# Order of loads and stores on SyncE's DMA queue in a PEER block: the activation store ahead of the next weight load

## The reference

```python
def chunk(ht):                       # 128 tokens
    q = (ht @ w_q).reshape(PEER_CHUNK, PEER_HEADS, 2, PEER_HALF)
    s = jnp.einsum('thpc,hpnc->thpn', q, subkeys)
    sv, si = lax.top_k(s, PEER_TOPK)
    ...                              # top 16 of the 16 x 16 sums per head -> expert, gate
    ue = u[expert]
    ve = v[expert]
    act = jax.nn.gelu(jnp.einsum('thkd,td->thk', ue, ht), approximate=False)
    return jnp.einsum('thk,thkd->td', (gate * act), ve)
```

## Time and profile before

| | us |
|---|---|
| median of 3 runs | 2909.25 |
| lowest, highest | 2909.18, 2910.72 |
| the profiled execution | 2909.18 |
| its span, first to last instruction | 2907.4 |
| TensorE (PE) busy | 2806.9, 97% |
| VectorE (DVE) busy | 1906.2, 66% |
| GpSimd (POOL) busy | 1549.0, 53% |
| ScalarE (ACT) busy | 901.7, 31% |

### The profile page before, as it was taken

The page is one execution under the profiler, slowest core; times in us unless marked ns, Lnnn a source line. Parts: engine busy times, 40 slices in busy tenths (PEclk is TensorE's granted clock), DMA queues, the critical chain, the costliest instruction groups (busy, mean ns, idle before and its releaser), DMA issues.

```text
span 2907.4 us, 44634 instructions
## 1 busy us (share of the span) xinstructions
PE 2806.9 (97%) x16719; PEld 2372.6 (82%) x16719; DVE 1906.2 (66%) x4442; ACT 901.7 (31%) x1750; POOL 1549.0 (53%) x1088
## 2 busy tenths in 40 slices
PE   7999989999999999999999998999999999999998
PEld 6777667999999999899999998666767766767675
DVE  6022363799888999999999743655555555555554
ACT  4223341322222222366666522222222222222222
POOL 1111020455666677755555563866656566666662
PEclk9999989999999999999999999999999999999999
DMA  3100031345777788899999996989999999899996
GB/s 137 44 30 30 23 131 73 102 144 208 264 271 281 262 274 289 293 360 373 379 381 381 369 344 255 338 303 336 332 332 337 334 322 327 314 333 319 324 324 231
DMA packets 300377, 763.51 MB, mean 263 GB/s; under 512 B 21456, under 2 KB 136528, under 8 KB 297424
## 3 DMA queue, kind: packets, MB, share of 16 engines
q0 software_dynamic: 110592, 402.70, 38.3%
q1 hardware_dynamic: 189648, 359.13, 34.7%
HBM read 669.47 MB, written 92.27 MB: 262 GB/s over the span
## 4 chain that ended last, share of the span: by engine, by line
PE 74%; DVE 8%; POOL 3%; DMA 1%; issue 1%; ACT 1%; ACTq 0%; DVEq 0%; POOLq 0%
PE bank L1832 30%; PE bank L1488 26%; PE wide L1852 6%; PE bank L1796 5%; PE bank L1707 3%; PE bank L1724 2%; POOL w_lo L602 1%; DVE u_row L1309 1%; DVE eq L1296 1%; DMA w_raw<-in_u 1%; PE bank L1733 1%; POOL u_row L611 1%; DVE eq L1294 1%; DVE route L1298 1%; POOL v_row L662 1%
## 5 line engine op out<-in xcount | busy, mean ns | idle before, releaser
L662 POOL DMA_INDIRECT v_row<-in_v,ids_t x384 | 381.6, 994 | 391.2 <-PE wide L1852 283.0
L1488 PE MATMUL bank<-h_hi,w_hi 128*128 128x320 f32 (+1 forms) x2400 | 574.3, 321 | 16.2 <-POOL w_lo L602 13.9
L1488 PE MATMUL bank<-h_hi,w_lo 128*128 128x320 f32 (+1 forms) x2400 | 557.1, 313 | 0.0
L1488 PE MATMUL bank<-h_lo,w_hi 128*128 128x320 f32 (+1 forms) x2400 | 557.1, 313 | 0.0
L1405 DVE TENSOR_TENSOR a_lo<-prod,a_hi 128x384 fp32r<-128x384 f32 (+1 forms) x256 | 264.0, 1031 | 445.4 <-ACT a_hi L969 445.2
L602 POOL TENSOR_TENSOR w_lo<-w_raw,w_hi 128x1024 fp32r<-128x1024 f32 x144 | 367.3, 2551 | 337.7 <-ACT w_hi L889 205.2
L1309 DVE CUSTOM_DVE_ANT_0 u_row<-wide,u_row 128x1024 f32<-128x1024 f32 x384 | 450.2, 1220 | 76.5 <-DMA u_row<-in_u_rows,ids 74.4
L611 POOL DMA_INDIRECT u_row<-in_u_rows,ids x384 | 390.7, 1017 | 113.4 <-issue 73.8
L1488 PEld LDWEIGHTS bank<-h_hi,w_hi 128*128 128x128 f32 x2400 | 400.5, 190 | 23.0 <-POOL w_lo L602 15.0
L1832 PE MATMUL bank<-v_hi,a_hi 128*128 128x512 f32 x1272 | 407.6, 402 | 10.4 <-POOL v_lo L651 5.3
L1488 PEld LDWEIGHTS bank<-h_lo,w_hi 128*128 128x128 f32 x2400 | 406.8, 189 | 4.0
(11 more groups left out here) (211 smaller groups left out, 3480.2 us busy)
## 6 DMA issues: line engine op xcount, KB each, us to landing
w_raw<-in_u SPq DMA_DIRECT2D x128, 512.0 KB, 5.4
v_raw<-in_v SPq DMA_DIRECT2D x32, 2048.0 KB, 19.6
act_d<-act_st SPq DMA_DIRECT2D x128, 320.0 KB, 5.3
g_d<-g_st SPq DMA_DIRECT2D x20, 2048.0 KB, 9.4
a_raw<-act_d SPq DMA_DIRECT2D x32, 768.0 KB, 8.1
g_raw<-g_d SPq DMA_DIRECT2D x32, 768.0 KB, 11.8
w_raw<-in_w_q SPq DMA_DIRECT2D x32, 512.0 KB, 3.4
a_raw<-act_d SPq DMA_DIRECT2D x32, 512.0 KB, 10.5
```

The source lines that it names most:

```text
L662: nc.gpsimd.indirect_dma_start(v_row[k % RING][:, :], None, v_rows, bass.IndirectOffsetOnAxis(ids_t[:, t, TW * s + c:TW * s + c + 1], 0)). ...
L1488: ins = pe.matmul(banks[h][:, 0:n], lhs[:, part], rhs[:, k, h * n:(h + 1) * n], start=(k == 0 and lhs is lhs_hi and rhs is h_hi), stop=(k ...
```

## The change

In SP's program a store used to be one item behind: for each t it issued the load of item t + 2 and then the store of item t - 1. Now it issues the load of item t + 2 and then the store of item t. The strip's store still stands right behind the activation store of the strip's second item. The loads of v, a and g stand behind both stores of their pair of items, one item later than before. The strips' part of SP's program is now a loop instead of 40 written-out items.

```diff
             load_item(0)
             load_item(1)
             for t in range(2 * BODY1):
                 load_item(t + 2)
-                if t:
-                    store_item(t - 1)
+                if query_of(t) is None:
+                    sp.wait_ge(act_done, 2 * t + 2)
+                    sp.dma_start(act_d[chunk_of(t)], act_st[:, t % 2, :]).then_inc(act_out[t % 2], 16)
+            def first_half(it, last=False):
+                for s in range(2):
+                    if not last:
+                        sp.wait_ge(lo_done, it * 2 + (W_U0 + s + 1))
+                        sp.dma_start(w_raw[:, s, :], u_d[it * 2 + (2 + s - Q_PIECES)]).then_inc(raw_in[s], 16)
+                    sp.wait_ge(act_done, it * 4 + (2 * s + 2))
+                    sp.dma_start(act_d[it * 2 + (s - Q_PIECES)], act_st[:, s, :]).then_inc(act_out[s], 16)
             with sp.Fori(BODY1, B0) as it:
-                for s in range(2):
-                    sp.wait_ge(lo_done, it * 2 + (W_U0 + s + 1))
-                    sp.dma_start(w_raw[:, s, :], u_d[it * 2 + (2 + s - Q_PIECES)]).then_inc(raw_in[s], 16)
-                    sp.wait_ge(act_done, it * 4 + 2 * s)
-                    sp.dma_start(act_d[it * 2 + (s - 1 - Q_PIECES)], act_st[:, 1 - s, :]).then_inc(act_out[1 - s], 16)
-            for t in range(2 * B0, 2 * C0):
-                load_item(t + 2)
-                store_item(t - 1)
-                if t % 2 == 0 and t > 2 * B0:
-                    store_strip(t // 2 - B0 - 1)
+                first_half(it)
+            with sp.Fori(0, PAIRS) as it:
+                for s2 in range(2):
+                    first_half(it * 2 + (B0 + s2))
+                    sp.wait_ge(gs_done, it * 16 + (8 * s2 + 8))
+                    sp.dma_start(g_d[it * 2 + s2], g_st[:, s2, :, :]).then_inc(g_out[s2], 16)
...
             for it in range(C0, ITEM_BODIES):
-                for t in (2 * it, 2 * it + 1):
-                    if t + 2 < ITEMS:
-                        load_item(t + 2)
-                    store_item(t - 1)
-                    if t == 2 * C0:
-                        store_strip(STRIPS - 1)
+                first_half(it, last=it == ITEM_BODIES - 1)
                 k = it - (ITEM_BODIES - 6)
                 if k in (0, 1):
                     load_v(0, k)
...
-            store_item(ITEMS - 1)
```

More of the change, by code:

```diff
@@ L472, in load_item @@
                 load_piece(W_U0 + t, u_d[chunk_of(t)] if hp is None else wq_d[hp])
[L474 to L478, removed]
             load_item(0)
@@ L483, in _ @@
                 load_item(t + 2)
-                if t:
-                    store_item(t - 1)
-            with sp.Fori(BODY1, B0) as it:
-                for s in range(2):
-                    sp.wait_ge(lo_done, it * 2 + (W_U0 + s + 1))
-                    sp.dma_start(w_raw[:, s, :], u_d[it * 2 + (2 + s - Q_PIECES)]).then_inc(raw_in[s], 16)
-                    sp.wait_ge(act_done, it * 4 + 2 * s)
-                    sp.dma_start(act_d[it * 2 + (s - 1 - Q_PIECES)], act_st[:, 1 - s, :]).then_inc(act_out[1 - s], 16)
-            def store_strip(st):
-                sp.wait_ge(gs_done, 8 * st + 8)
-                sp.dma_start(g_d[st], g_st[:, st % 2, :, :]).then_inc(g_out[st % 2], 16)
-            for t in range(2 * B0, 2 * C0):
-                load_item(t + 2)
-                store_item(t - 1)
-                if t % 2 == 0 and t > 2 * B0:
-                    store_strip(t // 2 - B0 - 1)
+                if query_of(t) is None:
[8 more added lines that the diff above has]
+                    sp.dma_start(act_d[it * 2 + (s - Q_PIECES)], act_st[:, s, :]).then_inc(act_out[s], 16)
+            with sp.Fori(BODY1, B0) as it:
+                first_half(it)
[4 more added lines that the diff above has]
+                    sp.dma_start(g_d[it * 2 + s2], g_st[:, s2, :, :]).then_inc(g_out[s2], 16)
             def load_v(g, s):
```

## The result

The changed kernel takes 2943.57 us (median of 4, 2940.6 to 2946.18) against 2909.22 (median of 4, 2906.33 to 2910.72). The ratio is 1.0119, 95% interval 1.0101 to 1.0137. It is slower, as forecast, but by 34 us and not by 12, and outside the range (2909 to 2932). The profiled execution took 2943.35, its span is 2941.6.

What follows compares the result with a forecast made beforehand. The prediction took TensorE to bound the item stage, with late transfers costing only past their slack. Plain items 0, strips 3.1 and v loads 8.5 made 11.6 us on 2909.18, so 2920.8 us, range 2909 to 2932.

Steps and rivals of the forecast that it cites:

- The bound and the thresholds: Item stage: TensorE bounds; L889 lateness costs only beyond 2.73 us in plain items, 3.36 us in strips.
- Plain items, cost 0: Plain items: the weight load makes L889 at most 2.5 us late, under 2.73, so nothing is lost.
- The rival by which they gain: Plain items before the strips: gathered rows land sooner, TensorE's 13.9 us of waiting shrink; 2902 us; 6%.
- The v loads, +8.5: End of item stage: weight loads behind two 2 MB v loads come late; 5.3 + 4.2 - 1.0 = +8.5 us.
- Its first term: First v load: the load behind it makes L889 7.99 us late, costing TensorE 5.26 us.
- Its second term: Second v load: the load behind it makes L889 late, loss 2.9 or 5.6 us, taken as 4.2.
- The strips, +3.1: Strips: loads behind strip stores cost 2.4 us in the first, 0.7 in the second, 0 in a settled one.
- Every strip stalls: Strips: each load 1.5 us later still, strips cost 10 us instead of 3.1, total 2928 us; 18%.
- The load overtakes: Loads right behind 2 MB transfers: they land in about 6 us, all terms vanish, 2908.2 to 2909.2 us; 18%.

Runs made afterwards that it cites:

- the run of its own: Kernel before with only the last 20 items, including the v, a and g loads, in the new order; 2912.08 us, ratio 1.0027.
- the strips' experiment, the first experiment: Kernel before with only the 20 strips in the new order, written out without a loop on SyncE; 2943.49 us, ratio 1.0133.
- new order, gathers pinned: Kernel before with only strips in the new order, plus GpSimd issuing an item's four gathers there before waiting for w_hi; 2991.51 us, ratio 1.0286.
- its control: Kernel before with only GpSimd's order in the strips changed, gathers issued before its wait for w_hi; 2993.05 us, ratio 1.0293.

## Why the prediction was wrong

*The bound and the thresholds.* Right. In the strip shown above L878 (once L889) was due when the gelus were through; its usual start is 0.63 us after theirs, at 1397.55. It started at 1402.73, x = 5.18, and 5.18 - 3.36 = 1.82 is TensorE's idle time of 1.80. The run with L889 behind a gate copy tests the same threshold.

*Plain items, cost 0.* Right: alone they measure a ratio of 0.9998. The rival by which they gain doesn't hold either.

*The v loads, +8.5.* The sum is near (+7.6 alone), but partly by luck. Its first term holds: the step that took 14.63 us for the load behind a v load from the earlier trace rows found 14.20, L889 waited 7.56 us where it was to be 7.99 late, and TensorE stood 4.79 where 5.26 was forecast (4.50 in the run of its own). Its second term, 4.2 us, measures nothing. The load behind the second v load was usable 1788.54 - 1775.45 = 13.09 us after it and not 14.63 to 17.37, and the item it was for came later than forecast, because TensorE ran at half its clock behind the first wait; L889 waited 1.39, under the threshold of 2.73. That slower stretch, 2.3 us, is what the forecast lacked, and it fills about half of the second term.

*The strips, +3.1.* Wrong, and this is the miss. The step that failed is "the load that is now issued 0.4 us behind the strip store lands when the load that followed that store landed before". For a settled strip that would have been 12.7 us after the store, x = 2.67 and under the threshold by 0.7. It came at a median 14.1 in the changed kernel and 14.8 in the strips' experiment, over the threshold in every settled strip of the latter, and a settled strip lost 1.8 to 2.0 us in the mean. The step kept the rest of the traffic where it stood, and it moves. This is GpSimd before the change (after the w_lo of the item, its gathers; strip store at 1402.46):

```profile
1393.60 2.39 POOL L602 TENSOR_TENSOR w_lo<-w_raw,w_hi 128x1024 fp32r<-128x1024 f32 x1 [3.31 <-DVE gate_j L1371]
...
1399.89 0.99 POOL L611 DMA_INDIRECT u_row<-in_u_rows,ids  x1 [0.31 <-issue]
```

and after it (strip store at 1411.52):

```profile
1403.93 2.38 POOL L591 TENSOR_TENSOR w_lo<-w_raw,w_hi 128x1024 fp32r<-128x1024 f32 x1 [5.94 <-ACT w_hi L878]
1406.46 1.23 POOL L600 DMA_INDIRECT u_row<-in_u_rows,ids  x1
...
1410.72 0.94 POOL L600 DMA_INDIRECT u_row<-in_u_rows,ids  x1 [0.30 <-issue]
```

A late L889 makes w_lo late, GpSimd issues its four gathers (2 MB) behind w_lo, and the last of them now starts 0.8 us ahead of the strip store, where it was 2.6. By this account they are still in the DMA engines' queues when the strip store comes, the load behind it lands later, and the next L889 is late again.

Medians of the settled strips, us; the last column is from the strip store's issue to its landing:

| run | last gather ahead of the store by | last load ahead by | store lands in |
|---|---|---|---|
| kernel before | 2.58 | 6.44 | 9.4 |
| strip store behind the load | 3.06 | 0.48 | 11.1 |
| kernel before, w_lo and gathers held back | 0.73 | 0.85 | 11.4 |
| new order, gathers ahead narrow | 2.55 | 10.6 | 7.8 |
| new order, gathers pinned | 3.08 | 12.5 | 8.6 |
| new order, gathers behind narrow | 1.35 | 11.6 | 12.4 |
| new order, L889 behind L917 | 0.68 | 10.6 | 11.5 |

In the four rows with the new order no load is near, and the store lands 3 to 5 us later where whole gathers start 0.7 to 1.4 us ahead of it than where they start 3.1 us ahead (in strips that are 3 to 4 us longer, though) or are narrow. For the strips' experiment and the changed kernel the profile has no landing, but it has the DMA engines' packets: the store's last packet ends 11.8 and 11.0 us after its issue, 8.9 before, and in that time 1.64 and 1.48 MB of gathers are moved, 0.97 before. The time order agrees as well. The first strip of the strips' experiment has no late L889 ahead of it, and its L889 comes 14.23 us after the store, earlier than the 15.79 of the forecast. From the second strip on it comes later than forecast: 15.83 for 14.15, then 13.7 to 15.6 for 12.7.

Taking the gathers ahead out takes the loss to zero, taking those behind out only from 39 to between 24 and 26 us. That the loop as a whole keeps itself up is put together from these links. The run that was to cut it by itself, with the gathers pinned, couldn't be read by its time since its control moved, and this was not tried in another way.

*The rivals.* "Every strip stalls" is what happened. It was given 18% and 10 us, and the strips cost 39. I gave it 1.5 us more per load, which is the size of the shift (14.1 to 14.8 for 12.7), but then let most strips off, since their loads had landed earlier than the settled one's. With the gathers moved, all strips behave alike: 39 us are 1.95 for each of the 20. "The load overtakes", for which a rule of the Trainium skill stood (DMA: Bandwidth & Descriptors, Queues, rings and completion order: completion "not FIFO per issuing engine"), shows nowhere here: in every strip of the first experiment L889 waited for the load behind the 2 MB. The section's own example is narrower than the use made of it here: a later transfer on one DMA engine behind one on sixteen. It also has each DMA engine report a transfer only after that engine's earlier writes, so it gives no reason for a load over all 128 partitions to be reported first. The same section says that a DMA engine takes turns between the queues that it has work for. That bears on gathers and strip store, which come by two queues. The packets of the kernel before show little of such turns at first: in the settled strips the store's first packet starts 2.8 us after its issue, while gathers are moved, and 1.3 us after it where the gathers are narrow. That the gathers ahead count so much more than those behind is measured here; how the engines come to it is open.

*The range.* It ended at 2932 because the strips' loss was bounded by what the rows show with the other traffic in its place.

## What to carry to other kernels

Before a load is moved right behind a large transfer on a DMA queue that works in order, compare its deadline with the time at which both will have landed. If the margin is only tenths of a microsecond, follow what the waiting engine issues next: when those are transfers for the same DMA engines, they move as well, and the margin was read with them in their old place. Here 0.7 us of margin stood against a shift of 1.4 to 2.1 us. Two cheap cures worked. One is an order in which the small urgent load goes first and the large patient transfer behind it (all of the strips' 39 us). The other is an in-order engine that does its short duties for others before it waits for a transfer (35 of the 39). And a wait of some microseconds on TensorE is priced with the slower clock behind it.

## What the runs showed of the hardware

Equal bytes taken from a strip are worth 39 us in front of the 2 MB store and 13 to 15 behind it. In the kernel before, the strip store lands in 9.4 us with the last gather 2.6 us ahead of it and the last load 6.4; with 512 KB issued 0.5 to 0.9 us ahead of it, it takes 11.1 to 11.5. A 512 KB load issued 0.5 us behind a 2 MB store was usable 14.8 us after that store's issue in the strips' experiment (median), and by 10.07 us at the latest where the gathers ahead were narrow. After TensorE stood idle for 4.5 and 4.8 us its granted clock was 0.50 for about 5 us of the matmuls that followed, which cost 2.3 us each time. Runs of the kernel before on one chip spread from 2898.07 to 2909.88 us, more than the 2909.18 to 2910.72 of its first three.
